# Other places in the engines' order for four small pieces of work inside three attention stages

## The reference

```python
# "ret": retention, 8 heads, q and k 128 wide, v and gate 256 wide
proj = rmsnorm(x, g_pre) @ w_in;  q, k, v, gate = split(proj)
scores = einsum('nbhcd,nbhmd->nbhcm', rope(q), rope(k)) * decay
o = groupnorm(scores @ v + cross)
x = x + rmsnorm((silu(gate) * o) @ w_out, g_post)
# "lat": latent attention, 8 heads
c_kv, k_r = split(rmsnorm(x, g_kv) @ w_kv_a); c_q, gate = split(rmsnorm(x, g_pre) @ w_in)
q, k_nope, v = rmsnorm(c_q) @ w_uq, rmsnorm(c_kv) @ w_uk, rmsnorm(c_kv) @ w_uv
p = softmax(mask(q_nope @ k_nope + rope(q_r) @ rope(k_r)) * scale)
x = x + rmsnorm((silu(gate) * (p @ v)) @ w_out, g_post)
# "dif": differential attention, 8 heads, two maps of 64 channels each
p = softmax(logits[0]) - lam * softmax(logits[1])       # logits = q @ k * scale + bias
o = rms_norm(p @ v, g_subln) * (1 - lambda_init)        # over the 128 channels of each head
x = x + rms_norm(o @ w_o, g_post_mix)
```

## Time and profile before

| | before |
|---|---|
| median of 3 runs | 2074.13 us (2072.65 to 2074.85) |
| the profiled execution's own time | 2073.53 us |
| its span | 2071.3 us, 2.2 us less than its time |
| TensorE, VectorE, ScalarE busy | 96%, 60%, 40% of the span |
| mean granted TensorE clock | 0.98 |
| moved by DMA | 179 MB, 86 GB/s on average |

### The profile page before, as it was taken

One profiled execution on the slowest core, in us unless ns is written; L12 is line 12 of the kernel. 1 busy time (PEld: TensorE's weight loads), 2 busy tenths in 40 slices (PEclk: granted clock), 3 DMA queues, 4 the chain that ended last, 5 costly groups with the idle time before them and its releaser, 6 DMA issues.

```text
span 2071.3 us, 27019 instructions
## 1 busy us (share of the span) xinstructions
PE 1979.0 (96%) x10458; PEld 1692.5 (82%) x10458; DVE 1242.5 (60%) x2179; ACT 832.3 (40%) x1381; POOL 316.0 (15%) x254
## 2 busy tenths in 40 slices
PE   7999999999889999999999999899998999999996
PEld 6888888887778887898888889787777988888895
DVE  6666566257555474457777624676664778774265
ACT  4233232344355433244444323445453544442342
POOL 3332232101132200110111100111010111110101
PEclk9999999999989999999999999989999999999997
DMA  4222222322210224232233322223111322233221
GB/s 157 99 77 87 88 70 76 96 92 85 72 31 31 83 92 130 81 97 95 87 102 102 122 97 76 82 74 105 60 42 62 88 86 94 93 109 116 98 73 50
DMA packets 53670, 179.00 MB, mean 86 GB/s; under 512 B 6151, under 2 KB 8711, under 8 KB 53544
## 3 DMA queue, kind: packets, MB, share of 16 engines
q1 hardware_dynamic: 53544, 177.29, 26.3%
HBM read 172.55 MB, written 4.72 MB: 86 GB/s over the span
## 4 chain that ended last, share of the span: by engine, by line
PE 65%; DVE 6%; ACT 3%; issue 2%; POOL 1%; POOLq 0%; DVEq 0%; ACTq 0%
PE pb L806 61%; DVE WL L789 1%; ACT WH L780 1%; PE pb L906 1%; PE pb L890 1%; PE pb L2585 1%; PE pb L2177 0%; PE pb L894 0%; ACT T L2727 0%; PE pb L1694 0%; DVE FR L2823 0%; DVE T L986 0%; DVE T L2864 0%; DVE FR L877 0%; POOL T L1292 0%
## 5 line engine op out<-in xcount | busy, mean ns | idle before, releaser
L806 PE MATMUL pb<-FR,WH 128*128 128x512 f32 (+1 forms) x5020 | 1450.5, 374 | 24.5 <-DVE WL L789 11.7
L806 PEld LDWEIGHTS pb<-FR,WH 128*128 128x128 f32 x5020 | 911.3, 190 | 189.6 <-DVE WL L789 11.7
L806 PE MATMUL pb<-FR,WL 128*128 128x512 f32 (+1 forms) x2510 | 933.3, 372 | 0.0
L789 DVE TENSOR_TENSOR WL<-stage,WH 128x1024 fp32r<-128x1024 f32 x311 | 401.8, 1310 | 414.4 <-ACT WH L780 413.5
L806 PEld LDWEIGHTS pb<-FR,WL 128*128 128x128 f32 x2510 | 476.8, 190 | 82.2
L780 ACT ACTIVATE WH<-stage 128x1024 fp32r<-128x1024 f32 x311 | 319.6, 1051 | 118.7 <-PE pb L806 106.0
L806 PE MATMUL pb<-WH,FR 128*128 128x256 f32 x832 | 155.9, 285 | 3.7 <-DVE T L1286 1.5
L806 PE MATMUL pb<-FR 128*128 128x256 f32 (+3 forms) x752 | 128.9, 324 | 20.9 <-DVE T L1493 12.2
L806 PEld LDWEIGHTS pb<-FR 128*128 128x128 f32 x752 | 117.3, 204 | 35.6 <-DVE T L1493 14.8
L806 PEld LDWEIGHTS pb<-WH,FR 128*128 128x128 f32 x832 | 131.6, 192 | 5.0 <-DVE T L1286 1.9
L1265 POOL TENSOR_TENSOR acc<-acc,T 128x512 f32<-128x512 f32 (+1 forms) x51 | 63.0, 1236 | 416.3 <-ACT T L1236 275.1
(11 more groups left out here) (222 smaller groups left out, 1674.9 us busy)
## 6 DMA issues: line engine op xcount, KB each, us to landing
stage<-in_ws SPq DMA_DIRECT2D x311, 512.0 KB, 3.5
X<-in_xT SPq DMA_DIRECT2D x8, 256.0 KB, 6.0
FD<-in_decay SPq DMA_DIRECT2D x8, 256.0 KB, 3.7
FD<-scr SPq DMA_DIRECT2D x1, 2048.0 KB, 8.4
out_dram<-X SPq DMA_DIRECT2D x8, 256.0 KB, 2.0
scr<-FD SPq DMA_DIRECT2D x10, 160.0 KB, 5.4
FD<-in_rope_b SPq DMA_DIRECT2D x2, 512.0 KB, 3.5
FD<-in_pT SPq DMA_DIRECT2D x4, 256.0 KB, 4.9
```

What stands on the lines that cost most here:

```text
L789: dve.tensor_tensor(lo, src, hi.bitcast(F32), ALU.subtract).then_inc(*self.tick("w_lo", ("w_lo", u)))
L806: m = pe.matmul(out, l, r, start=first and i == 0, stop=last and i == n - 1)
```

## The change

The same instructions are issued on every engine; some stand elsewhere. GpSimd's and SyncE's lists do not change at all.

1. `ret`: for heads 1 to 7 the second product of the second gate (L1312 before, in the new function `dve_gate_out`) moves behind that head's four products with the decays.
2. `lat`, reciprocals: for row block 2 the reciprocal (VectorE) and the division (ScalarE) move ahead of the next head's `query`; ScalarE's weight unit stays ahead of the division, VectorE's stays with the query, behind the reciprocal. In head 7 both move ahead of the weight units of the output projection.
3. `lat`, `value`: the copies out of the banks move ahead of the weight unit.
4. `dif`, `finish(h - 2)`: on TensorE, ScalarE and VectorE it moves ahead of scores(h, 2).
5. `dif`, weight units in odd heads: two units stood together ahead of `turn(h, 0)`. One now stands earlier (on ScalarE behind the unit of `key`, on VectorE ahead of `combine(h, 2)`), the other behind `turn(h, 2)`.

```diff
-    def dve_gate(self, dve, s, key, bank, g, r, reuse=None):
+    def dve_gate(self, dve, s, key, bank, g, r, reuse=None, later=False):
...
             *self.tick("gate_in", ("gate_in", s, *key), ("free", *bank)))
+        if not later:
+            self.dve_gate_out(dve, s, key, g)
+
+    def dve_gate_out(self, dve, s, key, g):
         t = ("t", s, "tanh", *key) if s == "lat" else ("t", s, "g", *key)
         dve.wait_ge(*self.at("tanh", s, *key))
         dve.scalar_tensor_tensor(out=g, in0=self.place[t], scalar=1.0, in1=g, op0=ALU.add, op1=ALU.mult).then_inc(
...
         for h in range(8):
             scores(h)
             if h:
+                self.dve_gate_out(dve, "ret", (h, 1), self.ret_gate_of(h, 1))
                 turn(h - 1)
...
-                    gate(h + 1, e)
+                    gate(h + 1, e, e == 1)
...
         def value(h):
+            self.act_natural(act, "lat", h, self.lat_vdst(h), ("lat", "kv"), ("pe", "lat", "pv", h - 2) if h else None)
             self.hi_to(act, BLOCK["w_uv", 1, h + 1])
-            self.act_natural(act, "lat", h, self.lat_vdst(h), ("lat", "kv"), ("pe", "lat", "pv", h - 2) if h else None)
...
             scores(h, 2)
             if after:
+                self.hi_to(act, BLOCK["w_uq", 2, nope_q(h + 1)])
+            divide(h, 2)
+            if after:
                 query(h + 1)
             else:
                 out("head 7, e")
-            divide(h, 2)
...
         def value(h):
+            self.dve_natural(dve, "lat", h, self.lat_vdst(h), ("lat", "kv"))
             self.lo_to(dve, BLOCK["w_uv", 1, h + 1])
-            self.dve_natural(dve, "lat", h, self.lat_vdst(h), ("lat", "kv"))
...
             scores(h, 2)
+            invert(h, 2)
             if after:
                 query(h + 1)
             else:
                 out("head 7, e")
-            invert(h, 2)
...
-                         h and {1: lambda: scores(h - 1, 1), 4: lambda: scores(h - 1, 2),
-                                5: lambda: h >= 3 and finish(h - 3)})
+                         h and {1: lambda: scores(h - 1, 1), 3: lambda: h >= 3 and finish(h - 3),
+                                4: lambda: scores(h - 1, 2)})
...
             if h % 2 == 0:
                 self.hi_to(act, BLOCK["w_kv_2", KD - 1, h])
+                if h:
+                    self.hi_to(act, BLOCK["w_kv_2", 3, 9 + h])
...
             scores(h, 1)
+            if h >= 2:
+                finish(h - 2)
             scores(h, 2)
...
             if h < 7:
                 c = (h + 1) // 2
-                if h % 2:
-                    self.hi_to(act, BLOCK["w_kv_2", KD - 1, 9 + 2 * c])
                 turn(h, 0)
                 turn(h, 1)
                 value(c, [(h + 1) % 2])
                 turn(h, 2)
-                if h % 2 == 0:
-                    self.hi_to(act, BLOCK["w_kv_2", KD - 1, h + 1])
+                self.hi_to(act, BLOCK["w_kv_2", KD - 1, 9 + 2 * c if h % 2 else h + 1])
...
             scores(h, 3)
+            c = (h + 1) // 2
+            if h % 2 and h < 7:
+                self.lo_to(dve, BLOCK["w_kv_2", 3, 9 + 2 * c])
             combine(h, 2)
             floor_of(h)
             if h < 7:
-                c = (h + 1) // 2
-                if h % 2:
-                    self.lo_to(dve, BLOCK["w_kv_2", KD - 1, 9 + 2 * c])
                 turn(h, 0)
                 turn(h, 1)
                 value(c, [(h + 1) % 2])
                 turn(h, 2)
+                if h % 2:
+                    self.lo_to(dve, BLOCK["w_kv_2", KD - 1, 9 + 2 * c])
```

More of the change, by code:

```diff
@@ L1474, in qk_out, with gate @@
             self.dve_rope(dve, "ret", (h, n), bank, self.ret_tab, ("tables", "ret"))
-        def gate(h, e):
+        def gate(h, e, later=False):
             bank = ("ret", "g", h, e) if h else ("ret", "w", 2 + e)
-            self.dve_gate(dve, "ret", (h, e), bank, self.ret_gate_of(h, e), ("r", "ret", "pre"))
+            self.dve_gate(dve, "ret", (h, e), bank, self.ret_gate_of(h, e), ("r", "ret", "pre"), None, later)
         def values_in(h):
@@ L2661, in pe_dif @@
                 scores(h, 1)
+                finish(5)
                 out("head 7, b")
@@ L2664, in pe_dif @@
                 out("head 7, c")
-                finish(5)
             scores(h, 3)
@@ L2707, in key @@
             if h >= 3:
-                finish(h - 3)
                 rounded(h - 3)
@@ L2836, in key @@
         def key(h):
-            if h >= 3:
-                finish(h - 3)
             if h % 2 == 0:
```

## The result

| | before | after |
|---|---|---|
| median | 2073.7 us (4 runs) | 2050.12 us (2049.05 to 2051.55, 4 runs) |
| the profiled execution: time, span | 2073.53, 2071.3 us | 2050.26, 2048.0 us |
| TensorE busy | 1979.0 us | 1973.0 us |
| span less TensorE busy | 92.3 us | 75.0 us |

The ratio is 0.9887, with an interval from 0.9869 to 0.9904: 19.9 to 27.2 us less. Forecast was 2050.0 (2044 to 2059). The changed kernel once more, in a later group, gave 2050.75 against 2072.35 for the kernel before, 21.6 us less.

The account below looks back on a forecast made before the run. TensorE was taken as the bound, busy 1979.0 of 2071.3 us, with 34.7 us of waits as ceiling for idle time. ret -12.4, lat -2.6 and dif -9.1 sum to -24.1: 2049.4, as median 2050.0 (range 2044 to 2059).

Parts of the forecast that it names:

- ret, the pause: ret, heads 1 to 7: TensorE's pause ahead of the decays falls from 1.57 to 0.25 us, 9.2 us in all.
- ret, the clock: ret: with pauses of 0.25 us both slow windows at clock 0.50 go, 3.2 us.
- lat, reciprocals: lat, block 2: next scores still wait for the query's chain through GpSimd, so 0; head 5 loses 0.9 us.
- lat, value: lat: 0.76 us each in heads 2 and 4, 0.8 in head 0, 1.2 for one slow window: -3.5 us.
- dif, units: dif, three odd heads: pauses of 1.32 us go, new ones of 0.7 come; net 0.6 each, -1.9 us.
- dif, the bank: dif: the earlier `finish` frees the bank that `values` writes; waits behind L2916 outside head 7 go, 3.3 us.
- dif, head 7: dif, head 7: one L2916 gained, 0.75 us; TensorE waits about 3 us for something of scores(7, 3) instead.
- The rival that the early `finish` stalls the softmax: dif: `finish` ahead of scores(h, 2) delays the maps and dif's 9.1 us is lost: 2059; chance 0.06.
- dif, the clock: dif: the stretch's two slow windows go with their pauses, 3.2 us.
- Outside: Stretches outside ret, lat and dif: no gain forecast, 0.
- The sign of slow windows where there were none: Whole kernel: the prediction counts as wrong if slow windows turn up where there were none.
- The rival of the clock: ret, lat, dif: falls of the clock move to other pauses, 7.6 us stay lost: about 2058; chance 0.15.

Follow-up runs that it names:

- the units alone: Only dif's two weight units of odd heads moved apart, `finish` left in place, on the kernel before: 2069.36 us, ratio 0.9984.
- reciprocals alone: Only lat's reciprocals and divisions of row block 2 moved ahead of the next query, on the kernel before: 2072.56 us, ratio 0.9994.
- value alone: Only value's copies moved ahead of the weight unit in lat, on the kernel before: 2067.88 us, ratio 0.9983.
- `finish` alone: Only the earlier `finish` in dif, without the units' move, on the kernel before: 2072.01 us, ratio 0.9996.
- the query early: Changed kernel, with lat's query for heads 1 to 7 moved ahead of its weight unit on VectorE and ScalarE: 2037.37 us, ratio 0.9827.
- ret alone: Only the ret part of the change, on the kernel before: 2059.19 us, ratio 0.9936.
- the longer pause: Kernel before, with an unread row maximum ahead of the second gate's first product in ret's heads 1 to 7: 2080.64 us, ratio 1.0041.

## Why the prediction was right, step by step

- *ret, the pause.* Forecast 0.25 us, measured 0.26, seven times; 9.2 us as said.
- *ret, the clock.* Both windows went, and ret reads 1.00. But the forecast took 3.2 us for them and the stage gave 11.25 - 9.2 = 2.1. In the last head TensorE now waits for GpSimd, 0.93 us in all, where the kernel before ran without such waits but at half clock. The timeline of the changed kernel there, and below it that of the units alone, which has the old code in ret and happened to have no slow window in its last head:

```profile
336.33 0.59 PE L806 MATMUL pb<-FR 128*128 128x256 f32 x3 [0.20 <-POOL FR L1590]
337.64 0.62 PE L806 MATMUL pb<-FR 128*128 128x256 f32 x3 [0.73 <-POOL FR L1590]
```

```profile
347.33 0.59 PE L806 MATMUL pb<-FR 128*128 128x256 f32 x3 [0.20 <-POOL FR L1585]
348.21 0.98 PE L806 MATMUL pb<-FR 128*128 128x256 f32 x6 [0.29 <-POOL FR L1585]
```

Reciprocals alone and value alone, with the old ret and no window in the last head either, have the same two waits; `finish` alone, with a window there, has none. So about 0.5 of the 0.93 us is work of GpSimd that the slow window had hidden, and the rest came as TensorE reaches this place 1.3 us sooner. The forecast had neither.

- *lat, reciprocals.* Right as a mechanism: the query's chain holds the next scores, shown from both sides, since reciprocals alone give nothing and the query early takes the wait away. Of the forecast -2.6 for lat, the -1.5 that the two profiles show is not shown to be the change's (see the result). Head 5 cost 1.0 (forecast 0.9). Not seen: 0.2 us more in the other heads, which is the reciprocal (0.17) ahead of the query.
- *lat, value.* The step that failed is "head 0: 0.8, and about 1.2 for one of the seven slow windows". The 0.8 went to the wait for the division, then for the query, and lat kept its windows, eight now for seven. Eight is also what ret alone has, with the old code in lat, so the eighth isn't put down to the edit. In heads 2 and 4 the pause that came back was 0.61 and 0.63 instead of 0.44. The timeline of head 2 in the changed kernel, against the earlier trace rows:

```profile
590.70 0.50 PE L806 MATMUL pb<-FR,WH 128*128 128x512 f32 x1 [0.61 <-DVE T L1286]
```

- *dif, units.* Right in direction, the new pause 0.42 instead of 0.7, so 2.7 instead of 1.9 us, but only with `finish` moved as well. VectorE at the end of head 3 and TensorE in front of head 4's scores, against the earlier trace rows:

```profile
1475.07 1.23 DVE L789 TENSOR_TENSOR WL<-stage,WH 128x1024 fp32r<-128x1024 f32 x1
...
1476.63 0.16 DVE L2907 SCALAR_TENSOR_TENSOR sm<-pb,sm 128x4 f32<-128x4 f32 x1
...
1476.85 0.62 PE L2592 MATMUL pb<-FR 64*128 64x256 f32 x6 [0.42 <-DVE sm L2907]
```

- *dif, the bank.* The 3.3 us went. TensorE now waits twice for a unit (L789) in this stage, 0.4 us in all, which the forecast had as hidden. It goes with the earlier `finish` and not with the moved units: `finish` alone has both waits (0.17 and 0.21), the units alone has none. With 2.7 + 3.3 - 0.4 and head 7's 1.6 the idle time of the stage is accounted for (7.2 of 7.3).
- *dif, head 7.* Forecast: one L2916 gained (0.75), and a wait of about 3 us for scores(7, 3). Measured: 3.72 + 0.61 + 0.69 + 0.82 = 5.8 before, 1.92 + 2.02 + 0.31 = 4.2 now, 1.6 us less, but the waits are not the ones named. The first is for the bias of scores(7, 2), which VectorE now does behind `finish`, the second for GpSimd's part of head 5's output. The rival that the early `finish` stalls the softmax is seen in the first, and in no other head:

```profile
1542.66 0.96 PE L2592 MATMUL pb<-FR 64*128 64x512 f32 x6 [1.92 <-DVE sm L2868]
...
1547.72 0.76 PE L806 MATMUL pb<-FR,WH 128*128 128x512 f32 x2 [2.02 <-POOL FR L3014]
```

- *dif, the clock.* Forecast two windows less; the trace of the kernel before has three in the whole stage, that of the changed one two, both behind the pause of 2.02. So 1.6 of the 3.2 us. That pauses and falls go together is shown for ret and lat; for dif it is not settled: with the old code in dif five profiles have two to four windows, with the new code five have two each, and over all profiles of this study there are one to six, and `finish` alone shows that they can eat 4.4 us of idle time.
- *Outside.* 2.0 us came from stretches that the change doesn't touch: 0.5 ahead of the first matmul of ret, 0.6 between ret and lat, 0.1 between lat and dif, 0.7 behind dif. They are no more than executions differ by. Over all fourteen profiles ret's first matmul starts between 59.3 and 61.0 us, and with the old code the stretch behind dif took 469.6 to 471.3 us. That they fell on the near side of the forecast is luck.
- *The sign of slow windows where there were none.* By its words the prediction has it against itself: the changed kernel has one behind the pause of 3.3 us at the start of lat, and a pair behind the pause of 2.02 in dif. The first stands behind the same pause in five profiles of other kernels (ret alone, reciprocals alone, value alone, the units alone, the longer pause), so it isn't put down to the change. The pair is: its pause is new, in a head where the kernel before has one window at the pause of 3.72.
- *The rival of the clock.* The Trainium skill's advice in "TensorE: Matmul & The Clock Gate", section "Why this matters for your kernels", on avoiding only longer gaps, is not borne out here: 10 falls behind 35 pauses of 1.57 us and 4 behind 7 of 2.17, none behind 56 shorter ones. The rival that the falls only move elsewhere fails within ret, where seven profiles with pauses of 0.26 us have none. Over the three stages ret alone has ten windows for twelve before (0, 8 and 2 for 2, 7 and 3). Whether lat's eighth is one that moved there is not shown.

## What to carry to other kernels

Where two waits stand one behind the other on the bounding engine, removing the first only renames the second; look for the end of the chain that the last one waits for (here a weight unit ahead of the query) and move that. An idle pause can cost more than its length, by the clock behind it, so compare busy times as well as waits, and take the ledger by stage between the same two instructions. A move that does nothing for idle time alone may pay once another has lifted the wait behind it: here the units, +0.2 us alone and -2.8 with `finish` moved. And before a small gain of one stage is believed, its length is to be compared over several profiles with the same code in it; in lat these differ by 1.6 us, as much as the gain was.

## What the runs showed of the hardware

- In ret, whose pauses lie some 42 us apart, pauses of TensorE of 0.26 and 0.78 us brought no fall of the granted clock (0 of 56), pauses of 1.57 us brought one in 10 of 35, pauses of 2.17 us in 4 of 7. The fall to 0.50 begins there 0.6 to 1.8 us behind the pause's end, and one costs 1.6 us.
- Which pause brings it differs between executions of the same code: in ret of the kernel before behind the pauses of heads 5 and 7, in the profile of value alone, with the same code there, behind those of heads 1, 4 and 6. The times of one kernel can come out in groups with different mean clocks: value alone in seven runs from 2067.1 to 2068.4 at 0.981 or 0.982, and in three from 2072.2 to 2072.7 at 0.980.
- A stretch at half clock can hide the work of another engine, so that removing it gives less than its 1.6 us. With the old code ret took 308.9 us with a window in head 5 alone, 309.8 with one more in the last head (0.9 us for it), and 310.6 and 312.1 with two and three in other heads (1.6 us each).
